# The next tile's input norm moved from the attention phase into the mLSTM phase of a hybrid encoder layer

## What is computed

```
h  = rms_norm(x, norm_g)                       # per token, 1024 features
mq, mk, mv, mo, mz, mi, mf, aq, ak, av, az, gm, ga = split(h @ w_in + b_in)
h_m = mlstm(silu(conv(mq, mk)), mv, mi, mf)    # causal matrix memory, state C, n, m
h_m = rms_norm(h_m, m_head_g) * sigmoid(mo)
h_a = band_attention(rms_norm(aq), rms_norm(ak), av)   # own chunk and 8 chunks back
u   = sigmoid(gm) * ((h_m * silu(mz)) @ w_bm) + sigmoid(ga) * ((h_a * silu(az)) @ w_ba)
y   = x + u @ w_out
```

## Time and profile before

| | us |
|---|---|
| median of 3 timed runs | 2293.7 (2286.06 to 2330.91) |
| the profiled execution, its own time | 2287.03 |
| its span, slowest core (core 7) | 2285.3 |
| spans of the 8 cores | 2267.5 to 2285.3 |
| PE matmuls busy in the span | 1652.9 |
| ACT busy | 864.5 |
| DVE busy | 767.4 |

### The profile page before, as it was taken

The page is one execution under the profiler, slowest core; times in us unless marked ns, Lnnn a source line. Parts: engine busy times, 40 slices in busy tenths (PEclk is TensorE's granted clock), DMA queues, the critical chain, the costliest instruction groups (busy, mean ns, idle before and its releaser), DMA issues.

```text
span 2285.3 us, 31291 instructions; the slowest of 8 cores (2267.5 to 2285.3 us)
## 1 busy us (share of the span) xinstructions
PE 1652.9 (72%) x9898; PEld 802.8 (35%) x9898; DVE 767.4 (34%) x1512; ACT 864.5 (38%) x1823; POOL 223.8 (10%) x377
## 2 busy tenths in 40 slices
PE   1556698667887597857773787598859785987677
PEld 0122343233433343335232233343334333433343
DVE  3114424233333324323222234324343434243322
ACT  2214544324342435324311335445334443444241
POOL 2001001110011000200010011000200020001101
PEclk9777798888899798966795888799979997989969
DMA  2662115951224222433344225122432243223504
GB/s 65 129 149 72 74 67 132 170 182 53 80 93 162 78 76 88 143 91 116 120 138 133 70 75 179 65 93 74 138 120 75 74 145 114 75 83 120 171 19 147
DMA packets 56843, 242.76 MB, mean 106 GB/s; under 512 B 7720, under 2 KB 11482, under 8 KB 36556
## 3 DMA queue, kind: packets, MB, share of 16 engines
q1 hardware_dynamic: 55628, 222.92, 29.5%
q0 software_dynamic: 1056, 17.86, 4.5%
HBM read 236.27 MB, written 40.17 MB: 121 GB/s over the span
## 4 chain that ended last, share of the span: by engine, by line
PE 45%; DMA 18%; ACT 13%; DVE 12%; issue 8%; POOL 2%; SPq 1%; DVEq 1%; ACTq 0%; POOLq 0%
DMA wscr<-w_all 6%; PE ps_pA L718 6%; DMA sb_ybuf<-x_p 6%; PE ps_pB L718 4%; PE ps_pA L1005 4%; PE ps_pB L680 4%; PE ps_pB L1005 4%; PE ps_pS L900 3%; PE ps_pA L680 2%; ACT sb_PT L906 2%; POOL sb_mixT L1030 2%; PE ps_pA L635 2%; PE ps_pG L1017 1%; PE ps_pX L891 1%; DVE sb_aqT L660 1%
## 5 line engine op out<-in xcount | busy, mean ns | idle before, releaser
L906 ACT ACTIVATE sb_PT<-ps_pS 128x512 bf16<-128x512 f32 x320 | 176.6, 593 | 193.4 <-PE ps_pS L900 191.8
L900 PE MATMUL ps_pS<-sb_aqT,sb_KTr 128*128 128x128 bf16 x1280 | 136.5, 256 | 95.6 <-ACT sb_PT L906 94.5
L718 PE MATMUL ps_pA<-sb_wbuf,sb_hT 128*128 128x512 bf16 (+1 forms) x680 | 171.9, 398 | 13.8 <-DVE sb_GA L754 6.5
L680 PE MATMUL ps_pB<-sb_hT,sb_wbuf 128*128 128x512 bf16 (+1 forms) x720 | 172.8, 387 | 0.0
L718 PE MATMUL ps_pB<-sb_wbuf,sb_hT 128*128 128x512 bf16 (+1 forms) x680 | 165.5, 387 | 0.1
L680 PE MATMUL ps_pA<-sb_hT,sb_wbuf 128*128 128x512 bf16 (+1 forms) x432 | 122.0, 437 | 33.9 <-DMA sb_wbuf<-wscr 30.5
L900 PEld LDWEIGHTS ps_pS<-sb_aqT,sb_KTr 128*128 128x128 bf16 x1280 | 96.2, 114 | 137.5 <-issue 132.2
L1005 PE MATMUL ps_pA<-sb_hT,sb_wbuf 128*128 128x512 bf16 (+1 forms) x576 | 132.4, 375 | 13.4 <-ACT sb_thg L1008 13.2
L1005 PE MATMUL ps_pB<-sb_hT,sb_wbuf 128*128 128x512 bf16 (+1 forms) x576 | 128.0, 366 | 10.2 <-ACT sb_thg L1008 8.4
L1030 POOL TENSOR_TENSOR sb_mixT<-sb_stage 128x512 bf16<-128x512 f32 (+1 forms) x72 | 82.9, 1151 | 348.1 <-DVE sb_stage L1027 328.0
L1017 PE MATMUL ps_pG<-sb_hmT,sb_wbuf 128*128 128x512 bf16 (+1 forms) x288 | 69.4, 363 | 49.8 <-DVE sb_stage L1024 49.6
(11 more groups left out here) (206 smaller groups left out, 2591.6 us busy)
## 6 DMA issues: line engine op xcount, KB each, us to landing
sb_wbuf<-wscr SPq DMA_DIRECT2D x153, 1024.0 KB
wscr<-w_all POOLq DMA_DIRECT2D x17, 1024.0 KB, 12.2
sb_xin<-x_p SPq DMA_DIRECT2D x32, 512.0 KB
sb_ybuf<-x_p SPq DMA_DIRECT2D x64, 256.0 KB
y_p<-sb_ybuf SPq DMA_DIRECT2D x64, 256.0 KB
v_p<-sb_scr_a SPq DMA_DIRECT2D x8, 256.0 KB
k_p<-sb_scr_a SPq DMA_DIRECT2D x8, 256.0 KB
sb_stage<-ck SPq DMA_DIRECT2D x8, 256.0 KB
```

Of the source, the lines that this page charges most:

```text
L680: S.op("pe", lambda e, pb=pb, wv=wv, kc=kc, c4=c4: e.matmul(pb[:, 0:NT], lhsT=wv[:, kc, c4 * 128:(c4 + 1) * 128], rhs=hTv[:, kc, 0:NT], st ...
L718: S.op("pe", lambda e, pb=pb, wv=wv, kc=kc, n=n, c0=c0: e.matmul(pb[0:n, :], lhsT=hTv[:, kc, c0:c0 + n], rhs=wv[:, kc, :], start=(kc == 0) ...
L900: S.op("pe", lambda e, h=h, slot=slot, kt=kt, bank=bank, idx2=idx2, c0=c0: e.matmul(pSS[bank][:, (idx2 % 4) * 128:(idx2 % 4 + 1) * 128], l ...
L906: S.op("act", lambda e, nb=nb, bank=bank: e.activation(out=PT[:, nb * 512:(nb + 1) * 512], in_=pSS[bank][:, :], func=AF.Exp, scale=0.125), ...
```

## The change

`g_xp` is split into `g_x` (the norm of a tile) and `g_xp2` (the start of a sequence, the gates and the early projections). `g_g` is split into `g_ga` (gates of both halves and the first half's projections, in their old order) and `g_gb` (the second half's projections and the output units). The new function `merged` takes one step of each of two generators in turn. Phase M of tile i now runs `g_m` against `g_pl`, `g_ga` of tile i-1, and then `g_gb` of tile i-1 merged with `g_x` of tile i+1. Phase A runs `g_a` against `g_xp2`, which has 27 steps for a prompt tile where `g_xp` had 39. In tile 0, where there is no tile i-1, the norm follows `g_pl`. Tile 8 has no successor, and its phases keep their order. No instruction is added or removed. `g_x` of tile i+1 writes the same `hT` buffer as `g_ga` of tile i-1 reads, and stands behind it.

```diff
--- before.py
+++ after.py
@@ -471,7 +471,7 @@
             hak = [f"haT{j}" for j in range(nsub)]
             cur_slot = ti % 2 if kind == "p" else 1
 
-            def g_xp():
+            def g_xp2():
                 if first:
                     for g in groups:
                         gi = g["gi"]
@@ -492,6 +492,9 @@
                     if kind == "p":
                         S.op("pool", lambda e: e.memset(C_f[:], 0.0), writes=["C_f"])
                     yield
+                yield from g_xp2_rest()
+
+            def g_x():
                 for j, su in enumerate(subs):
                     n = su["n"]
                     xb = xi_i[0] % 2
@@ -520,6 +523,8 @@
                                                                       in1=bc(gx[:], [128, 8, n], 2), op=ALU.mult),
                          reads=["pT", "gx"], writes=[hTk[j]])
                     yield
+
+            def g_xp2_rest():
                 deferred = []
                 for gsel, (pb, pk) in enumerate([(pA, "pA"), (pB, "pB")]):
                     for kc in range(8):
@@ -993,8 +998,17 @@
                          reads=["pT"], writes=[hak[j]])
                     yield
 
-            def g_g():
-                for hf in range(2):
+            def g_ga():
+                yield from g_g_in(0)
+                yield from g_g_u(0)
+                yield from g_g_in(1)
+
+            def g_gb():
+                yield from g_g_u(1)
+                yield from g_g_out()
+
+            def g_g_in(hf):
+                if True:
                     for which, (nm, boff, toff) in enumerate([(f"gm{hf}", 16, 0), (f"ga{hf}", 24, 4)]):
                         wt, wk = use_piece(nm)
                         wv_ = v3(wt[:], 8)
@@ -1009,6 +1023,9 @@
                                                                                                   bias=bfm_h[:, bch:bch + 1], scale=0.5),
                                  reads=[pk, "bfm_h"], writes=[f"thg{toff + d4}"])
                             yield
+
+            def g_g_u(hf):
+                if True:
                     wbt, wbk = use_piece(f"wb{hf}")
                     wbp = wbt[:].rearrange("p (m c d) -> p m c d", m=2, c=4)
                     for d4 in range(4):
@@ -1030,6 +1047,8 @@
                         S.op("pool", lambda e, dc=dc: e.tensor_tensor(out=mixv[:, dc, 0:NT], in0=scr_g1[:, 0:NT], in1=scr_g2[:, 0:NT], op=ALU.add),
                              reads=["scr_g1", "scr_g2"], writes=[f"mix{dc}"])
                         yield
+
+            def g_g_out():
                 yield
                 yield
                 units = [(eh, j) for eh in range(2) for j in range(nsub)]
@@ -1068,7 +1087,7 @@
                     ld(yo, ybv[0:n, yb, :], [], rk=[yk])
                     yield
 
-            T.xp, T.pl, T.m, T.a, T.g = g_xp, g_pl, g_m, g_a, g_g
+            T.x, T.xp2, T.pl, T.m, T.a, T.ga, T.gb = g_x, g_xp2, g_pl, g_m, g_a, g_ga, g_gb
             return T
 
         EARLY = ["mq", "mk", "mv", "mo", "mz"]
@@ -1115,15 +1134,34 @@
                 except StopIteration:
                     c["alive"] = False
 
-        interleave([[tiles[0].xp]])
+        def merged(gfa, gfb):
+            def gf():
+                a, b = gfa(), gfb()
+                alive = [a, b]
+                while alive:
+                    for g in list(alive):
+                        try:
+                            next(g)
+                            yield
+                        except StopIteration:
+                            alive.remove(g)
+            return gf
+
+        interleave([[tiles[0].x, tiles[0].xp2]])
         for i, T in enumerate(tiles):
-            bulk = [T.pl, tiles[i - 1].g] if i > 0 else [T.pl]
+            nxt = tiles[i + 1] if i + 1 < NTL else None
+            bulk = [T.pl]
+            if i > 0:
+                bulk.append(tiles[i - 1].ga)
+                bulk.append(merged(tiles[i - 1].gb, nxt.x) if nxt else tiles[i - 1].gb)
+            elif nxt:
+                bulk.append(nxt.x)
             interleave([[T.m], bulk])
-            if i + 1 < NTL:
-                interleave([[T.a], [tiles[i + 1].xp]])
+            if nxt:
+                interleave([[T.a], [nxt.xp2]])
             else:
                 interleave([[T.a]])
-        interleave([[tiles[-1].g]])
+        interleave([[tiles[-1].ga, tiles[-1].gb]])
         assert piece_pos[0] == len(piece_seq), (piece_pos[0], len(piece_seq))
         S.emit()
     return nc
```

## The result

The changed kernel takes 2363.5 us (median of 10 executions), the kernel before 2287.4 us (10) on the same chip: a ratio of 1.033 [1.030, 1.035], slower. The forecast was 2276, in a range from 2185 to 2340.

A forecast was written before the change was run, and what follows sets the result against it. The prediction took the kernel as bound by PE in some stretches and by waits in others. Phase A gives back 138 us, phase M pays 120, net 18: 2287.0 to 2269, with 6.7 for the timed median 2276; range 2185 to 2340.

The forecast's parts named there:

- both are small as long as PE runs groups of eight 512-column matmuls in between; I take 20 us: Phase A, ordinary tile: uncovered gates and more frequent Exp waits cost little, so moving the norm saves 20 us.
- Work and slow clock: Phase M's tail: the norm's transposes add 4.2 us on PE, slow matmuls after two longer waits 3.5 us.
- First slice: Phase M's tail: x loads behind wout1's weights, the merge's second step waits for its scaling, PE idles 8.8 us.
- Second slice: Phase M's tail: load early, but transposes stand in `pT` behind the mLSTM's own and ACT's copy, about 2.3 us.
- Third and fourth: Phase M's tail: each slice's load stands behind a store of y; PE idles 3 us and 5 us.
- Hidden waits of `ybuf`: Phase M's tail: of 8.9 us that DVE already waits for `ybuf` loads, 7 are hidden by its later arrival.
- Relief in front: Phase M: 4.9 of 36 mLSTM steps move from the front into the tail, freeing 2.5 us in front.
- are not longer than what I have: Tile 5's phase M: four slices at 5.8 us cost no more than an ordinary tile's 17 us.
- (a): Rival: waits overlap and phase M's tail absorbs the norm, paying 7 instead of 17 us a tile: 2210; chance 0.33.
- (b): Rival: phase M's tail loses the clock, running at 0.55 throughout, a tile paying 31 us: 2360; chance 0.11.
- (c): Rival: attention's own chain paces the head of phase A, each A giving 8 us instead of 20: 2348; chance 0.06.
- The signs: Wrong if first x load issues well before PE ends ga1, tail is outside 45 to 60 us, or A gives under 14.

The follow-up runs named there:

- e6: The changed kernel with two more empty steps between `ha` and its transposes in phase A: 2310.4 us, 1.011 of the kernel before.
- e10: The kernel before with only two more empty steps between `ha` and its transposes: 2257.0 us, 0.989.
- e3: The changed kernel with x loaded ahead: first two slices behind the late projections, later ones behind the scaling that frees their buffer: 2281.5 us, 0.999.
- e4: The kernel before with only the x loads of the next tile's first two slices issued ahead, behind phase M's late projections: 2247.3 us, 0.984.
- e12: The changed kernel (norm moved) with x loaded ahead and two more empty steps before the transposes of `ha`: 2231.8 us, 0.976.
- e13: The kernel before (norm unmoved) with x loaded ahead and two more empty steps, on the same chip as e12: 2231.2 us, 0.977.
- e8: e4 with `ybuf` loads three units ahead of use, each later one behind the store that frees its buffer: 2273.9 us, 0.996.

## Why the prediction was wrong, point by point

**The step that failed first: "both are small as long as PE runs groups of eight 512-column matmuls in between; I take 20 us".** The attention that remains was costed at PE's 91% of before, though I had written that a projection now comes only every 68/27 steps and not every 68/39. An ordinary A gave 12.4 us and not 20; with tiles 0 and 3 (4.2 and 2.6 us, forecast 14 and 4) the seven phases gave 68.7 and not 118. From the first projection on, PE idles 13 us of an A where it idled 6.4, and the difference sits at the transposes of `ha`, 9.0 us a tile against 2.5 before. I expected it, if at all, at the wait for Exp, and that one fell (76.4 to 39.2 us in five phases). e6 shows what this wait costs in the changed kernel: two steps of distance take 31.7 us off it and 32.5 off five phases, down to 93.6 us each. But e10 gets 22.9 us from the same steps without the move, so most of e6's gain was open to the kernel before too, and against a like kernel the move gives 14.3 us in A. Why it is not 20 even then stays open. 49 of the 85 us by which the net was missed lie in phase A.

**The terms of the tail were right in kind, low in sum.** In tile 7 I had 19.8 us for the tail without the relief in front; it is 25.1 (58.9 - 33.8).
- Work and slow clock, forecast 4.2 + 3.5: PE is busy 33.23 us in place of 25.12, 8.1 more. Over the five whole M's it is 9.8 a tile, 6 of it the clock.
- First slice, forecast 8.8: 8.33.
- Second slice, forecast 2.3: 3.01 + 1.50 = 4.5. I had taken only the durations of the mLSTM's chain and not that DVE reaches it late.
- Third and fourth, forecast 3 and 5: 4.24 and 6.33. The loads took 4.5 and 4.9 us from issue to square, where I had 4.0, and DVE and ACT another 2.8 to the transposes.
- Hidden waits of `ybuf`, forecast 7: PE's idle time in the tail rose by 25.7 - 8.7 = 17.0 us, the four waits make 23.4, so 6.4 were hidden.
- Relief in front, forecast 2.5: none, 92.3 us against 92.1.

**Tiles 1 and 5 were not ordinary.** Their phases M pay 29.7 and 32.4 us. In the last 60 us of tile 1's M PE waits 8.5 us for the merge and 11.6 for the scaling, as in tile 7, and the granted clock is 0.74; the last 29 us before had 1.00. For tile 5 I had argued that its four slices "are not longer than what I have". In its last 63 us PE waits 10.7 us for `hmT` of the mLSTM at a transposition of the norm, and 10.1 for the merge; the sample tile's merge and output are probably too short to fill these, which no run shows. Tiles 2, 6 and 7 pay 22.4, 18.1 and 24.5. Tile 0 paid 4 (forecast 12), tile 3 11 (forecast 6). The seven M's pay 142 where 103 was forecast, 39 us of the miss, and by e3 the late loads are 13.8 us of each ordinary one: the price of an M, 17 us forecast and 25.4 measured, was the second term that was mis-sized. Tile 4's own M and A came to -2.4 together, forecast -3.

**The rivals.** (a), the waits overlap, did not happen: each of the four stands apart in the timeline. (b), the tail loses the clock, gave nearly the measured time, 2360, but not by its mechanism: the granted clock of tile 7's tail is 0.80, not below the 0.59 from which it decides, and the slow matmuls cost some 4 us and not 21. After the waits of 8.3 and 6.3 us the next groups took 1.87 us for four and 3.26 for eight, where 1.02 and 1.89 are those at full clock, and after the third slice's wait one group took 2.84 us and the next 1.89 again. The rule of the Trainium skill (TensorE: Matmul & The Clock Gate, HAM oscillation) is that bursts between DMA waits start at the lower clock. The trace agrees behind the waits of 8.3, 4.2 and 6.3 us, but the tail does not stay low. My "longer than about 3 us" rested on a single wait, 3.65 us; the next longest of that tail was 1.45. (c), the head of A is not freed, is nearest to what happened: it had 8 us of gain in A and the load as the only thing in its way. The gain is 12.4, the head itself came free (15.1 us, forecast 12), and the time came back further on in the phase.

**The signs.** Of the three that were to show me wrong one came: phase A gave less than 14 us. The first load was not issued before PE ended ga1, and the tail took 58.9 us, within 45 to 60.

**What I had not asked** is what the late load costs with the norm left where it is. e4 answers it: some 37 us for moving two loads. A term of "20 us saved by moving the norm" held 8.5 that needed no move, and e12 and e13 show that, once loads and steps are right, the move is worth nothing measurable, in either direction, to within some 6 us.

## What to carry to other kernels

Before moving work to get rid of a stall, move the load that the stall waits for: here that alone gave 37 us, where 18 was forecast for the whole change, and the moved work took its late load with it. Where two chains of steps are interleaved by count, taking steps out of one changes every distance between producer and consumer in the other; count how much of the other chain's work stands in each gap before and after, for each wait, not only the longest. Try such a change of distance on the kernel before as well: here it helped there too. The best versions found, 0.974 to 0.979 of the time before, come from loading x ahead and from two empty steps, with the norm in either place.

## What the runs showed of the hardware

A store's flight counts against a queue that is in order: with `ybuf` loads issued behind the stores that free their buffers, SP stood 129.5 us in 40 waits of up to 6.5 us (e8), where it had stood 6.2 us in 7 (e4). Three 512 KB loads of x with other transfers around them took 5.6, 4.5 and 4.9 us from issue to the start of the square (1931.75 to 1937.36, behind 1 MB of weights; 1960.43 to 1964.97; 1974.84 to 1979.72). The Trainium skill (DMA: Bandwidth & Descriptors, Anatomy of one DMA) would have a lone one land in 3.2, by an estimate from its 2.0 us fixed and 436 GB/s. Its figures are for loads issued by GpSimd and these are issued by SP, a difference that the prediction passed over; no run here has such a load alone, and in this kernel's traffic the estimate is 1.3 to 2.4 us short.
